# Residual parked in memory during the experts stage, its SBUF room used as a second buffer for one up matrix

## The chip, the cores and the metric

The kernel runs on one core of one Trainium2 chip. The metric is the device time of one execution in microseconds (us), as a median over runs. TensorE, VectorE, ScalarE and GpSimd are called PE, DVE, ACT and POOL in profile rows. SP is the engine whose queue issues nearly all transfers, and PS is the accumulator memory (PSUM).

## The reference, cut to what matters

The program is three blocks on one sequence of T = 512 tokens of width D = 1024, all in float32. The change lies in the last part of the first block, the mixture of experts:

```
x = x + gt1 * hybrid_mixer(...)                  # the residual
h = modulate(rmsnorm(x, g_norm2), sh2, sc2)
g = argmax(softmax(h @ w_rg + b_rg))             # one group of 4
e = top_k(softmax((h @ w_re + b_re)[g]), 2)      # two of its 8 experts
y[t] = sum_e w[t,e] * ((silu(h_t @ w_gate[e]) * (h_t @ w_up[e])) @ w_down[e])
x = x + gt2 * y                                  # the residual is needed again
x = rmsnorm(x, g_final)
```

There are 32 experts, each with a gate (1024 x 512), an up (1024 x 512) and a down matrix (512 x 1024), 2 MB each, so the stage reads 192 MB of weights, whatever the routing. Two more blocks follow (a gated delta rule with a feed-forward part, and an attention with one).

## The kernel before

**Pairs.** The experts stage works on two experts at a time. `PAIRS` is 16, and a hardware loop on each engine runs over "doubles", two pairs a turn (q = 0 and q = 1), eight turns for these inputs. For a pair PE does, in order: the gate product (`main_of`, line 874, 32 matmuls for two times 64 rows; `rest_of`, line 883, 32 for 32 more rows of the first expert), the up product (the same two lines), some transposes (lines 905, 864, 867 and 910, of the hidden rows and of the next pair's tokens), and the down product (line 919, 32 matmuls, and line 926, 32). Each ends with an increment of `m_pc`, six a pair: gate main, gate rest, up main, up rest, down main, down rest. `m_done(i, step)` is the value that `m_pc` has behind a step of pair i.

**Buffers.** A is one tensor of 59 rows of 512 floats per partition; an expert matrix takes eight rows. Gate matrices have two sets of buffers (lines 303 and 304): A[8:16] and A[16:24] for q = 0 and the two slots of `ring` for q = 1. Up matrices have one set, A[0:8] and A[32:40], and down matrices one set, A[24:32] and `h`. x is an SBUF tensor of 2 MB that holds the residual; during the stage nobody reads or writes it.

**Order of transfers.** SP issues all expert matrices from one queue. Ahead of the stage (lines 472 to 488): both gates of pair 0, the ups of pair 0, the first gate of pair 1 and the first down of pair 0; then the four writes of the token rows to `h2_tokens` (line 484, each behind its `ht_ev`); then a wait for the gathers of the token rows of pairs 0 and 1 (`xg`, line 486), the second down of pair 0 and the second gate of pair 1. In the loop (lines 508 to 522) each group of loads waits on `m_pc` until PE is through with the product that used the buffer: the gates of pair p+2 behind the gate product of pair p, the ups of p+1 behind the up product of p, the downs of p+1 behind the down product of p. PE waits for `wg`, `wu` and `wd` ahead of each product (lines 892, 899, 915).

**POOL** gathers token rows from `h2_tokens` for each pair by indirect DMA (line 2608) behind the `f_tok` semaphore, and writes finished rows to `y_assignments` (line 2646).

**Behind the stage** (lines 528 to 538) SP waits for the last hidden rows (`m_sg`) and gathers, loads `w_ab` and the first two weight units of the next block into `ring`, waits for the last writes of `y_assignments` (`sc0`, `sc1`), and loads these rows in four parts of 1 MB (line 538). DVE first takes the low parts of the first unit (line 2213), weighs and adds the rows part by part (lines 2224 and 2225), PE transposes them (line 933), and DVE adds them to the residual (line 2233): `x = PS * mod + x`.

Of the kernel before, what the change touches and what calls it, by code (L numbers as in the profile page):

```python
# [19 lines left out]
F32 = mybir.dt.float32  # L20
# [3 lines left out]
P = 128  # L24
D = 1024
T = 512
KD = D // P
NT = T // P
# [123 lines left out]
def build(nc, xt_in, wada, wall, wexp, w_if, w_router, w_ab, vecs, rows, b_if, cst_in, ints, att_bias, out_t):  # L152
    f_tok = nc.dram_tensor("h2_tokens", [T, D], F32, kind="Internal").ap()
    y_asg = nc.dram_tensor("y_assignments", [2 * T, D], F32, kind="Internal").ap()
    slots = nc.dram_tensor("slot_table", [SLOT_COLS * P, 2], I32, kind="Internal").ap()

    ctx = ExitStack()
    with ctx:
        def sb(name, shape, dt=F32):
# [4 lines left out]
        def S(name):  # L164
            if name not in sems:
                sems[name] = ctx.enter_context(nc.semaphore(name))
            return sems[name]
# [15 lines left out]
        h = sb("h", [P, KD, T])  # L183
        ring = sb("ring", [P, 2, 8, 512])
        A = sb("A", [P, 59, 512])
        x = sb("x", [P, KD, T])
# [113 lines left out]
        token_scale = A[:, 23, :]  # L300


        moe_up, moe_dn = [A[:, 0:8], A[:, 32:40]], [A[:, 24:32], h[:]]
        moe_gate = [[A[:, 8:16], A[:, 16:24]], [ring[:, 0], ring[:, 1]]]
        xg = [[A[:, 40:42, :], A[0:QUARTER, 42:44, :]], [A[:, 55:57, :], A[0:QUARTER, 57:59, :]]]
        x_main, x_rest = A[:, 44:46, :], A[:, 46, 0:KD * QUARTER]
# [13 lines left out]
        def m_done(i, step):  # L320

            return PRODUCTS * i + (step + 1)

        def rwait(eng, sem, value):

            eng.wait_ge(sem, value)
            eng.sem_inc(S("waits"), 1)
# [92 lines left out]
        def _(sp):  # L420
# [42 lines left out]
            def gate_of(q, j, e):  # L463
                sp.dma_start(moe_gate[q][j], e[:, 0].rearrange("a p k n -> p (a k) n")).then_inc(S(f"wg{q}{j}"), 16)

            def up_of(j, e):
                sp.dma_start(moe_up[j], e[:, 1].rearrange("a p k n -> p (a k) n")).then_inc(S(f"wu{j}"), 16)

            def down_of(j, e):
                sp.dma_start(moe_dn[j], e[:, 2].rearrange("a p k n -> p (a k) n")).then_inc(S(f"wd{j}"), 16)  # L470
# [1 line left out]
            sp.wait_ge(S("mm"), TILE_DONE[G_MOUT + 1][3])  # L472
            gate_of(0, 0, wexp[0:1])
            gate_of(0, 1, wexp[1:2])
            up_of(0, wexp[0:1])
            sp.wait_ge(S("merged"), KD)
            up_of(1, wexp[1:2])
            sp.wait_ge(S("mm"), UNIT_USED["w_out0"])
            gate_of(1, 0, wexp[2:3])
            sp.wait_ge(S("mm"), UNIT_USED["w_out1"])  # L480
            down_of(0, wexp[0:1])
            for t in range(NT):
                sp.wait_ge(S("ht_ev"), t + 1)
                sp.dma_start(f_tok[t * P:(t + 1) * P, :], A[:, 40 + 2 * t:42 + 2 * t, :].rearrange("p a b -> p (a b)")).then_inc(S("f_tok"), 16)
            for q in range(2):
                sp.wait_ge(S(f"xg{q}"), 32)
            down_of(1, wexp[1:2])
            gate_of(1, 1, wexp[3:4])

            n = doubles(sp)  # L490
            m = doubles_less_one(sp)
# [11 lines left out]

            def ups(es):
                for j in range(2):
                    up_of(j, es[j])

            with sp.Fori(1, n) as d:
                done = 2 * PRODUCTS * d
                before, first, second = experts(2 * d - 1), experts(2 * d), experts(2 * d + 1)  # L510
                rwait(sp, S("m_pc"), done + m_done(-2, 1))
                gates(0, first)
                rwait(sp, S("m_pc"), done + m_done(-2, 3))
                ups(before)
                rwait(sp, S("m_pc"), done + m_done(-2, 5))
                downs(before)
                rwait(sp, S("m_pc"), done + m_done(-1, 1))
                gates(1, second)
                rwait(sp, S("m_pc"), done + m_done(-1, 3))
                ups(first)  # L520
                rwait(sp, S("m_pc"), done + m_done(-1, 5))
                downs(first)
            last = experts(2 * m + 1)
            rwait(sp, S("m_pc"), 2 * PRODUCTS * m + m_done(0, 3))
            ups(last)
            rwait(sp, S("m_pc"), 2 * PRODUCTS * m + m_done(0, 5))
            downs(last)
            rwait(sp, S("m_sg"), 8 * n)
            for q in range(2):
                rwait(sp, S(f"xg{q}"), 32 * n + 32)  # L530
            sp.dma_start(wab[:], w_ab).then_inc(S("small2"), 16)
            for u in range(NU1, NU1 + 2):
                sp.dma_start(ring[:, u % 2], wall[u]).then_inc(S(f"unit{u % 2}"), 16)
# [44 lines left out]
        def _(pe):  # L578
# [75 lines left out]
            for k in range(KD):  # L654
                pe.wait_ge(S("h_lo"), k + 1)
                last = product(PS[0:64, 4, :], (wif_hi[:, k, :], wif_lo[:, k, :]), (x_r[:, k, :], h_r[:, k, :]), k == 0, k == KD - 1)
# [33 lines left out]
            for g in range(10):  # L690
# [3 lines left out]
                for j in range(4):  # L694
                    p = 4 * g + j
# [7 lines left out]
                    if j < 2 and g in (0, 2, 4, 8):  # L703
                        n = (0, 2, 4, 8).index(g)
# [165 lines left out]
            def main_of(bank, w):  # L870

                for k in range(KD):
                    for j in range(2):
                        last = mm(PS[HALF * j:HALF * (j + 1), bank, :], x_main[:, k // 4, (k % 4) * P + HALF * j:(k % 4) * P + HALF * (j + 1)],  # L874
                                  w[j][:, k, :], start=k == 0, stop=k == KD - 1)
                last.then_inc(S("m_pc"), 1)

            def rest_of(w):

                for k in range(KD):  # L880
                    for half in range(2):
                        g = HALF * (k % 2) + QUARTER * half
                        last = mm(PS[g:g + QUARTER, 5, 0:256], x_rest[:, k * QUARTER:(k + 1) * QUARTER], w[0][:, k, 256 * half:256 * (half + 1)],  # L883
                                  start=k < 2, stop=k >= KD - 2)
                last.then_inc(S("m_pc"), 1)

            rows_T(0, 32)
            n = doubles(pe)
            with pe.Fori(0, n) as d:
                for q in range(2):  # L890
                    for j in range(2):
                        pe.wait_ge(S(f"wg{q}{j}"), 16 * d + 16)
                    pe.wait_ge(S("m_x"), 4 * d + (2 * q + 1))
                    main_of(3, moe_gate[q])
                    pe.wait_ge(S("m_x"), 4 * d + (2 * q + 2))
                    pe.wait_ge(S("m_y1"), 2 * d + (q + 1))
                    rest_of(moe_gate[q])
                    for j in range(2):
                        pe.wait_ge(S(f"wu{j}"), 32 * d + 16 * (q + 1))
                    main_of(4, moe_up)  # L900
                    pe.wait_ge(S("m_h"), 8 * d + (4 * q + 1))
                    rest_of(moe_up)
                    pe.wait_ge(S("m_h"), 8 * d + (4 * q + 2))
                    for k in range(4):
                        last = nc.tensor.transpose(PS[:, 3, k * P:(k + 1) * P], hid_main[:, k * P:(k + 1) * P], ident)
                    last.then_inc(S("m_tr"), 1)
                    rows_T(1 - q, 32 * d + 32 * (q + 1))
                    rwait(pe, S("m_h"), 8 * d + (4 * q + 4))
                    for k in range(2):
                        last = nc.tensor.transpose(PS[:, 4, k * HALF:(k + 1) * HALF], hid_rest[:, k * P:(k + 1) * P], ident[0:HALF, 0:HALF])  # L910
                    last.then_inc(S("m_tr"), 1)
                    pe.wait_ge(S("m_ht"), 2 * d + (q + 1))
                    pe.wait_ge(S("m_y0"), 2 * d + (q + 1))
                    for j in range(2):
                        pe.wait_ge(S(f"wd{j}"), 32 * d + 16 * (q + 1))
                    for half in range(2):
                        for k in range(4):
                            for j in range(2):
                                last = mm(PS[HALF * j:HALF * (j + 1), 6 + half, :], hT_main[:, k * P + HALF * j:k * P + HALF * (j + 1)],  # L919
                                          moe_dn[j][:, 4 * half + k, :], start=k == 0, stop=k == 3)  # L920
                    last.then_inc(S("m_pc"), 1)
                    pe.wait_ge(S("m_hr"), 2 * d + (q + 1))
                    for k in range(4):
                        at = HALF * (k % 2) + QUARTER * (k // 2)
                        for t in range(4):
                            last = mm(PS[QUARTER * t:QUARTER * (t + 1), 5, 256:512], hT_rest[:, at:at + QUARTER],
                                      moe_dn[0][:, 4 * (t // 2) + k, 256 * (t % 2):256 * (t % 2 + 1)], start=k == 0, stop=k == 3)
                    last.then_inc(S("m_pc"), 1)
# [858 lines left out]
        def _(dve):  # L1787
# [240 lines left out]
            for m in range(2):  # L2028
                for j in range(4):
                    q = 8 + 4 * m + j  # L2030
# [162 lines left out]
            n = doubles(dve)  # L2193
# [32 lines left out]
            def a_lo(k):  # L2226

                dve.wait_ge(S("h_hi"), KD * (1 + MIX_SETS) + k + 1)
                stt(h_r[:, k, :], x[:, k, :], gm[:, 0, k:k + 1], h_hi_r[:, k, :].bitcast(F32), ALU.mult, ALU.subtract).then_inc(S("h_lo"), 1)

            for k in range(KD):
                dve.wait_ge(S("yT"), k + 1)
                stt(x[:, k, :], PS[:, k, :], mod[:, 40 + k:41 + k], x[:, k, :], ALU.mult, ALU.add).then_inc(S("xt"), 1)
                if k:
                    dve.wait_ge(S("xt"), KD + k)
                    a_lo(k - 1)
# [535 lines left out]
```

## Time and profile before

| | |
|---|---|
| median of 3 runs | 2365.41 us (2361.35 to 2365.88) |
| the profiled execution | 2357.39 us, of it the span 2355.5 us |
| PE busy | 2184.1 us (93%), mean granted clock 0.961 |
| DVE, ACT, POOL busy | 1212.3, 821.6, 107.0 us |
| moved by DMA | 384.62 MB, mean 163 GB/s |
| experts stage | roughly 470 to 966 us of the span |

In the rows below times are us from the start of the span; PEclk is the TensorE clock that was granted, as a share of 2.4 GHz, and the DMA share is the mean busy share of the core's 16 DMA engines.

### The profile page before, as it was taken

The page shows a single profiled execution, that of the slowest core. Times are in us where ns is not written, and L with a number is a line of the kernel's source. Part 1 is how long each engine was busy: PE and PEld are TensorE (multiplying, and loading weights), DVE is VectorE, ACT ScalarE, POOL GpSimd, SP SyncE. Part 2 cuts the span into 40 slices and gives each one's busy share as a digit, 9 for nine tenths or more (in the row PEclk, how much of TensorE's full clock was granted, in tenths as well). Part 3 has the DMA queues.
Part 4 walks back from the last instruction along what each step waited for, and adds up shares of the span by engine and source line. Part 5 has one row for each costly group of instructions (what it writes and reads, how often), then busy time and mean ns, then how long its engine had stood idle before and what let it go on. Part 6 is the DMA issues. An engine that isn't in the chain of part 4 may idle for free.

```text
span 2355.5 us, 30115 instructions
## 1 busy us (share of the span) xinstructions
PE 2184.1 (93%) x11752; PEld 1567.1 (67%) x11752; DVE 1212.3 (51%) x1813; ACT 821.6 (35%) x1494; POOL 107.0 (5%) x135
## 2 busy tenths in 40 slices
PE   7999998899998999799994989999999899999997
PEld 3788757633333343367783977888887677888885
DVE  4899576400000000457747446778525654877822
ACT  3222353233322333443552433223324454222421
POOL 0000000021111111000002000000000000000000
PEclk9999999899999999899996899999999899999999
DMA  9442104599999998511210112322223102222221
GB/s 393 169 179 77 71 33 164 201 387 428 426 426 424 418 418 354 206 72 72 72 37 1 37 58 86 107 77 102 108 107 112 68 1 96 84 107 107 76 104 72
DMA packets 34455, 384.62 MB, mean 163 GB/s; under 512 B 8112, under 2 KB 8384, under 8 KB 11456
## 3 DMA queue, kind: packets, MB, share of 16 engines
q1 hardware_dynamic: 27520, 374.96, 40.0%
q0 software_dynamic: 6848, 8.45, 1.0%
q8 instruction: 60, 0.98, 0.2%
q14 instruction: 27, 0.22, 0.0%
HBM read 382.59 MB, written 14.73 MB: 169 GB/s over the span
## 4 chain that ended last, share of the span: by engine, by line
PE 74%; DMA 13%; DVE 8%; ACT 4%; issue 2%; SPq 0%; DVEq 0%; ACTq 0%; POOL 0%; POOLq 0%
PE PS L646 19%; PE PS L647 18%; PE PS L648 18%; DMA A<-wexp 11%; PE PS L874 6%; PE PS L883 2%; DVE A L1903 1%; PE PS L919 1%; DMA x<-xt_in 1%; PE PS L1049 1%; PE PS L599 1%; PE PS L606 1%; PE PS L964 1%; PE PS L1242 1%; PE PS L626 0%
## 5 line engine op out<-in xcount | busy, mean ns | idle before, releaser
L647 PE MATMUL PS<-h_r,w_hi_r 128*128 128x512 f32 x1104 | 434.3, 393 | 0.0
L646 PE MATMUL PS<-h_hi_r,w_hi_r 128*128 128x512 f32 x1056 | 425.4, 403 | 8.9 <-DVE A L1903 3.4
L2213 DVE TENSOR_TENSOR ring_r<-ring,w_hi_r 128x1024 fp32r<-128x1024 f32 x196 | 238.7, 1223 | 345.1 <-ACT w_hi_r L1506 344.9
L648 PE MATMUL PS<-h_hi_r,ring_r 128*128 128x512 f32 x1056 | 414.9, 393 | 0.0
L1506 ACT ACTIVATE w_hi_r<-ring 128x1024 fp32r<-128x1024 f32 x196 | 206.2, 1058 | 567.9 <-PE PS L648 335.9
L646 PEld LDWEIGHTS PS<-h_hi_r,w_hi_r 128*128 128x128 f32 x1056 | 200.6, 190 | 63.5 <-issue 11.0
L647 PEld LDWEIGHTS PS<-h_r,w_hi_r 128*128 128x128 f32 x1104 | 210.3, 191 | 47.4 <-issue 4.8
L648 PEld LDWEIGHTS PS<-h_hi_r,ring_r 128*128 128x128 f32 x1056 | 200.8, 190 | 42.8
L874 PE MATMUL PS<-A 128*64 128x512 f32 x768 | 174.9, 609 | 25.9 <-DMA A<-wexp 23.9
L1903 DVE SCALAR_TENSOR_TENSOR A<-A,vec 128x511 f32<-128x511 f32 (+15 forms) x216 | 160.2, 742 | 6.7
L2198 DVE TENSOR_TENSOR A<-A,PS 64x256 f32<-64x256 f32 x16 | 6.6, 413 | 280.3 <-ACT A L1482 280.3
L874 PEld LDWEIGHTS PS<-A 128*64 128x64 f32 x768 | 59.6, 140 | 130.5 <-issue 128.4
L647 PE MATMUL PS<-hid_r,w_hi_r 128*128 128x512 f32 x352 | 136.9, 389 | 0.0
L646 PE MATMUL PS<-x_r,top_r 128*128 128x512 f32 x320 | 127.6, 399 | 5.6 <-DVE ring_r L1813 5.6
L647 PE MATMUL PS<-h_r,top_r 128*128 128x512 f32 (+1 forms) x328 | 128.9, 393 | 0.0
L648 PE MATMUL PS<-x_r,ring_r 128*128 128x512 f32 x320 | 125.8, 393 | 0.0
L919 PE MATMUL PS<-A 128*64 128x512 f32 x256 | 113.2, 595 | 0.3 <-DMA h<-wexp 0.3
L919 PE MATMUL PS<-h,A 128*64 128x512 f32 x256 | 113.3, 595 | 0.0
L1331 ACT ACTIVATE top_r<-ring 128x1024 fp32r<-128x1024 f32 x40 | 42.4, 1060 | 161.8 <-PE PS L648 161.8
L648 PE MATMUL PS<-h_r,ring_r 128*128 128x512 f32 x224 | 87.8, 392 | 0.0
L646 PE MATMUL PS<-top_r,w_hi_r 128*128 128x512 f32 x208 | 80.9, 389 | 0.0
L648 PE MATMUL PS<-top_r,ring_r 128*128 128x512 f32 x208 | 80.9, 389 | 0.0
(478 smaller groups left out, 3409.5 us busy)
## 6 DMA issues: line engine op xcount, KB each, us to landing
A<-wexp SPq DMA_DIRECT2D x64, 2048.0 KB, 15.8
ring<-wall SPq DMA_DIRECT2D x63, 2048.0 KB, 8.1
ring<-wexp SPq DMA_DIRECT2D x16, 2048.0 KB, 18.2
h<-wexp SPq DMA_DIRECT2D x16, 2048.0 KB
A<-wada SPq DMA_DIRECT2D x12, 2048.0 KB, 14.6
x<-xt_in SPq DMA_DIRECT2D x2, 2048.0 KB, 10.4
A<-y_assignments SPq DMA_DIRECT2D x4, 1024.0 KB, 7.8
h_tokens<-A SPq DMA_DIRECT2D x4, 512.0 KB, 3.0
```

The source lines that it names most:

```text
L599: mm(PS[:, bank, :], ones, sq[:, k % 2, :], start=k == 0, stop=k == KD - 1).then_inc(S("sq_used"), 1)
L606: last = mm(PS[g:g + QUARTER, NORM_BANK[n], :], ones[:, 0:QUARTER], A[:, k, :], start=k < 4, stop=k >= 4)
L646: mm(out, w[0], x_[0], start=first, stop=False)
L647: mm(out, w[0], x_[1], start=False, stop=False)
L648: return mm(out, w[1], x_[0], start=False, stop=last_)
L874: last = mm(PS[HALF * j:HALF * (j + 1), bank, :], x_main[:, k // 4, (k % 4) * P + HALF * j:(k % 4) * P + HALF * (j + 1)], w[j][:, k, :], s ...
L883: last = mm(PS[g:g + QUARTER, 5, 0:256], x_rest[:, k * QUARTER:(k + 1) * QUARTER], w[0][:, k, 256 * half:256 * (half + 1)], start=k < 2, s ...
L919: last = mm(PS[HALF * j:HALF * (j + 1), 6 + half, :], hT_main[:, k * P + HALF * j:k * P + HALF * (j + 1)], moe_dn[j][:, 4 * half + k, :], ...
L1331: a_(in_hi(p), ring[:, g % 2, :, j * P:(j + 1) * P], ACT.Copy).then_inc(S("w_hi"), 1)
L1506: a_(w_hi_r[:, :, j * P:(j + 1) * P], ring[:, slot, :, j * P:(j + 1) * P], ACT.Copy).then_inc(S("w_hi"), 1)
L1903: ins = stt(dst[:, s:T], src[:, 0:T - s], w(j), dst[:, s:T], ALU.mult, ALU.add)
L2213: tt(ring_r[:, slot, :, cols], ring[:, slot, :, cols], w_hi_r[:, :, cols].bitcast(F32), ALU.subtract).then_inc(S("w_lo"), 1)
```

## The change

The residual x is written to a DRAM tensor `x_kept` ahead of the token rows. Its room becomes the up buffer of the first expert for q = 1; the second expert's up matrix stays in A[32:40] for both q. Ahead of the loop SP now also loads the first up matrix of pair 1. In the loop the first up matrix of the following odd pair is issued right behind the ups of the even pair, so ahead of that even pair's downs; at the odd pair's turn only the second up matrix is loaded. Behind the stage x is read back, ahead of `w_ab`, and DVE waits for it before it adds.

```diff
+    x_kept = nc.dram_tensor("x_kept", [P, KD, T], F32, kind="Internal").ap()
...
-        moe_up, moe_dn = [A[:, 0:8], A[:, 32:40]], [A[:, 24:32], h[:]]
+        moe_up, moe_dn = [[A[:, 0:8], A[:, 32:40]], [x[:], A[:, 32:40]]], [A[:, 24:32], h[:]]
...
-            def up_of(j, e):
-                sp.dma_start(moe_up[j], e[:, 1].rearrange("a p k n -> p (a k) n")).then_inc(S(f"wu{j}"), 16)
+            def up_of(q, j, e):
+                sp.dma_start(moe_up[q][j], e[:, 1].rearrange("a p k n -> p (a k) n")).then_inc(S(f"wu{j}"), 16)
...
             down_of(0, wexp[0:1])
+            sp.wait_ge(S("xt"), KD)
+            sp.dma_start(x_kept, x[:]).then_inc(S("x_in"), 16)
             for t in range(NT):
                 sp.wait_ge(S("ht_ev"), t + 1)
...
             gate_of(1, 1, wexp[3:4])
+            sp.wait_ge(S("x_in"), 48)
+            sp.wait_ge(S("ht_mm"), NT)
+            up_of(1, 0, wexp[2:3])
...
             def ups(es):
                 for j in range(2):
-                    up_of(j, es[j])
+                    up_of(0, j, es[j])
...
                 rwait(sp, S("m_pc"), done + m_done(-2, 3))
-                ups(before)
+                up_of(1, 1, before[1])
...
                 rwait(sp, S("m_pc"), done + m_done(-1, 3))
                 ups(first)
+                up_of(1, 0, second[0])
                 rwait(sp, S("m_pc"), done + m_done(-1, 5))
                 downs(first)
...
             rwait(sp, S("m_pc"), 2 * PRODUCTS * m + m_done(0, 3))
-            ups(last)
+            up_of(1, 1, last[1])
...
+            sp.dma_start(x[:], x_kept).then_inc(S("x_in"), 16)
             sp.dma_start(wab[:], w_ab).then_inc(S("small2"), 16)
...
-                    main_of(4, moe_up)
+                    main_of(4, moe_up[q])
                     pe.wait_ge(S("m_h"), 8 * d + (4 * q + 1))
-                    rest_of(moe_up)
+                    rest_of(moe_up[q])
...
+            dve.wait_ge(S("x_in"), 64)
             for k in range(KD):
                 dve.wait_ge(S("yT"), k + 1)
                 stt(x[:, k, :], PS[:, k, :], mod[:, 40 + k:41 + k], x[:, k, :], ALU.mult, ALU.add).then_inc(S("xt"), 1)
```

## Rows read from the trace of the kernel before

**Rows 1.** The page: the span in 40 slices, and the chain that ended last.

```profile
PE   7999998899998999799994989999999899999997
DMA  9442104599999998511210112322223102222221
GB/s 393 169 179 77 71 33 164 201 387 428 426 426 424 418 418 354 206 72 72 72 37 1 37 58 86 107 77 102 108 107 112 68 1 96 84 107 107 76 104 72
PE 74%; DMA 13%; DVE 8%; ACT 4%; issue 2%; SPq 0%; DVEq 0%; ACTq 0%; POOL 0%; POOLq 0%
```

**Rows 2.** Waits of PE, 484 to 960 us: waited for, us in total, times, longest.

```profile
PE PS L874 <- DMA A<-wexp: 23.9, 12, 3.2
PE PS L919 <- DMA h<-wexp: 0.3, 1, 0.3
```

**Rows 3.** Timeline of PE: start, us, what [idle before <-releaser].

```profile
570.95 7.09 PE L874 MATMUL PS<-A 128*64 128x512 f32 x32 [0.87 <-DMA A<-wexp]
...
726.32 7.09 PE L874 MATMUL PS<-A 128*64 128x512 f32 x32 [2.84 <-DMA A<-wexp]
...
822.45 8.78 PE L874 MATMUL PS<-A 128*64 128x512 f32 x32 [3.06 <-DMA A<-wexp]
...
853.83 7.09 PE L874 MATMUL PS<-A 128*64 128x512 f32 x32 [0.63 <-DMA A<-wexp]
...
865.40 0.61 PE L919 MATMUL PS<-A 128*64 128x512 f32 x1 [0.29 <-DMA h<-wexp]
...
917.30 7.09 PE L874 MATMUL PS<-A 128*64 128x512 f32 x32 [2.27 <-DMA A<-wexp]
...
928.51 0.64 PE L919 MATMUL PS<-A 128*64 128x512 f32 x1
```

**Rows 4.** Timeline of SP's queue: issues of transfers.

```profile
895.20 0.85 SPq L467 DMA_DIRECT2D A<-wexp  x2
906.41 0.33 SPq L470 DMA_DIRECT2D A<-wexp  x1
906.92 0.33 SPq L470 DMA_DIRECT2D h<-wexp  x1
926.52 0.86 SPq L467 DMA_DIRECT2D A<-wexp  x2
...
956.39 0.90 SPq L533 DMA_DIRECT2D ring<-wall  x2
971.25 0.80 SPq L538 DMA_DIRECT2D A<-y_assignments  x2
```

**Rows 5.** Windows: us, busy of PE, PEld, DVE, ACT, POOL, PEclk, DMA share, GB/s.

```profile
482.00:484.00 2.00, 2.00 (x30) 0.76 (x22) 0.38 (x1) 0.38 (x1) 0.00 (x0) 1.00 0.67 275
484.00:486.00 2.00, 2.00 (x12) 0.70 (x10) 0.04 (x1) 0.42 (x1) 0.89 (x2) 1.00 0.72 123
486.00:488.00 2.00, 2.00 (x12) 0.72 (x10) 0.00 (x0) 0.00 (x0) 0.24 (x1) 1.00 0.57 238
...
492.00:568.00 76.00, 76.00 (x550) 30.36 (x546) 5.57 (x13) 28.49 (x75) 15.13 (x21) 1.00 1.01 426
568.00:918.00 350.00, 325.81 (x2392) 134.41 (x2392) 24.86 (x56) 110.95 (x289) 47.90 (x68) 0.99 1.01 423
918.00:922.00 4.00, 4.00 (x20) 1.55 (x18) 0.00 (x0) 0.00 (x0) 0.00 (x0) 1.00 0.41 164
922.00:926.00 4.00, 4.00 (x44) 1.63 (x40) 0.69 (x1) 0.00 (x0) 0.00 (x0) 1.00 0.11 45
926.00:927.00 1.00, 1.00 (x15) 0.82 (x8) 0.27 (x1) 0.51 (x2) 0.00 (x0) 1.00 0.00 0
...
968.00:970.00 2.00, 0.00 (x0) 0.00 (x0) 0.00 (x0) 1.97 (x3) 0.90 (x1) 1.00 0.49 162
```

**Rows 6.** Issue and landing of the second gate of pair 1, issued at 471.40 us.

```profile
ring<-wexp SPq DMA_DIRECT2D x1, 2048.0 KB, 13.4
```

**Rows 7.** Landing of the token-row write issued last, at 454.57 us; POOL's first gather behind it.

```profile
h_tokens<-A SPq DMA_DIRECT2D x1, 512.0 KB, 3.2
463.95 1.24 POOL L2608 DMA_INDIRECT A<-h_tokens,idx  x1 [122.31 <-DVE idx L2156]
```

**Rows 8.** Timeline of DVE behind the stage, the first part of the rows.

```profile
976.08 0.75 DVE L2224 TENSOR_SCALAR A<-A,wtok 128x1024 f32<-128x1024 f32 x1 [0.42 <-DMA A<-y_assignments]
```

More of the change, by code:

```diff
@@ L474, in _ @@
             gate_of(0, 1, wexp[1:2])
-            up_of(0, wexp[0:1])
+            up_of(0, 0, wexp[0:1])
             sp.wait_ge(S("merged"), KD)
-            up_of(1, wexp[1:2])
+            up_of(0, 1, wexp[1:2])
             sp.wait_ge(S("mm"), UNIT_USED["w_out0"])
```

## The prediction

> **What bounds the kernel now.** I read the page first. Over the whole span PE is busy and carries 74% of the chain, but the slices around the experts are different: the DMA engines stand at 9 tenths and 387 to 428 GB/s for eight slices [rows 1]. So one stage of a PE kernel is bound by transfers. The windows confirm it: from 568 to 918 us the share is 1.01 at 423 GB/s [rows 5]. In PE's waits, every idle stretch from 484 to 960 us is a wait for an expert matrix: 12 waits for an up matrix, 23.9 us, and one of 0.3 us for a down matrix [rows 2]. From 492 to 568 us PE is busy throughout, although the share is already 1.01 [rows 5]: there PE is the slower one and lives on what was loaded ahead. The first wait stands at 570.95, the last at 917.30 us [rows 3], and from the last up product on PE runs through to the stage's end. Between those two starts lie eleven pairs, 66 matrices, in 346.35 us: **5.25 us a matrix**, token rows and results included. So the stage's end is set by when the up matrices of pair 14 land and by the PE work behind them.
>
> The queue is worked off in order. The ups of pair 14 were issued at 895.20 and let PE start at 917.30; the downs, issued at 906.41 and 906.92 [rows 4], were still moving at 922 to 926 us, with a share of 0.11, which is under two of 16 engines, and at 926 to 927 nothing moved [rows 5]. Two readings follow: a matrix counts as landed when the slowest engine is through, some 7 us behind the others, and downs land about 8.8 us behind ups at the tail. The Trainium skill (DMA: Bandwidth & Descriptors, Queues, rings and completion order) says that each engine consumes a queue's descriptors in ring order and that the semaphore needs all of them; the tail agrees.
>
> A down matrix has almost no slack. Pair 12's ups let PE start at 853.83, and its down product started at 865.40 after a wait of 0.29 us [rows 3]: PE needs the downs 11.2 to 11.5 us after it starts the ups (928.51 - 917.30 = 11.21 in pair 14), and two matrices behind the ups take 2 x 5.25 = 10.5.
>
> **The change, part by part.**
>
> *The write of x* (2 MB, SBUF to memory) stands in the queue ahead of the token-row writes. Its wait on `xt` is over at about 445 us, when x is final, and the first token write is issued at 451, so SP itself loses nothing. On the engines it costs 4.9 us (2.1 MB at 423 to 428 GB/s). The last token write landed at 454.57 + 3.2 = 457.8; with the write in front, at 462.7. POOL's gather started at 463.95, released by DVE's indices about 1 us earlier [rows 7]. Cost 0, hidden by the routing arithmetic; the cover is 0.3 us, so the bound above is what is left if writes run slower: 0 to +2, and a rival beyond it. The Trainium skill (DMA: Bandwidth & Descriptors, Anatomy of one DMA) warns that the receipt of a write to HBM dominates a transfer's fixed time; it speaks against a write in front of others here, but the 3.2 us of a 512 KB write in rows 7 holds that already.
>
> *The first up matrix of pair 1, loaded ahead.* It follows the second gate of pair 1, which landed at 471.40 + 13.4 = 484.8 [rows 6]. The next loads, the gates of pair 2, began to move after 485; the windows from 482 to 488 show shares of 0.67, 0.72 and 0.57 at 275, 123 and 238 GB/s [rows 5]. The idle room that the early load can use is between 1.4 us (slowest engine, my estimate from the landing less its receipt) and 2.9 us (bytes missing from 482 to 488 against 423 GB/s). I take 1.4, since landings go by the slowest engine. Everything behind it shifts by 5.25 - 1.4 = +3.9 us (2.3 to 4.9).
>
> *What this does in the saturated loop.* Counting matrices ahead of each product from 484 us on: ahead of any pair's **ups** the queue now carries one matrix less than before, so they land 5.25 - 3.9 = 1.4 us earlier. Ahead of an even pair's **downs** it carries as many as before (one went ahead of the stage, but the next odd pair's first up matrix was put in front of them), so these land 3.9 us later. Ahead of an odd pair's downs one less: 1.4 earlier. The early lead therefore buys nothing where it counts: the even downs, with 0 to 2.6 us of slack (landed by about 925.9, used at 928.51), become the wait that decides. Each even pair then waits about 3 x 5.25 - 11.3 = 4.5 us for its downs, and the waits on ups go nearly to nothing. The engines stay fed: each group of loads is still issued several us before the queue runs dry, so the period per pair stays 31.5 us.
>
> *The last even pair, 14.* Its downs landed at 925.9 and now land at 925.9 + 3.9 = 929.8, PE starts them at 930.0: **+1.5 us**. From the other side: ups at 915.8 and three matrices behind them, at the tail's 4.4 us 929.0, at 5.25 us 931.6, so +0.5 to +3.1. All behind is PE work that no longer waits (pair 15's second up and downs have 10 us to spare), so it shifts by the same.
>
> *The clock.* A wait of 2.84 us or less left the next 32 matmuls at 7.09 us, one of 3.06 made them 8.78: the clock had fallen from 2.4 to 1.2 GHz, 1.69 us [rows 3]. In pairs 4 to 12 the longer waits will do this with no cost, DMA being the bound. In pair 14 the wait is 930.0 - (915.9 + 11.2) = 2.9 us, on the edge. I charge half, **+0.85** (0 to +1.7).
>
> *Reading x back.* 2 MB go ahead of `w_ab` and two ring units, issued at 956.0 to 957.3 [rows 4]. These were through at about 969.3 (share 0.49 in 968 to 970) [rows 5] and will be at 974.2. The parts of the rows are issued at 971.25, began to move at about 972.4, and DVE took the first at 976.08, after a wait for it of 0.42 [rows 8]; now they begin at 974.4. **+2.0 us**, between 0 (if the engines take them in between) and the whole 4.9. ACT splits the first unit at 969.5, which then has just landed: 0. DVE's new wait on `x_in` is met by then: 0.
>
> *PE, DVE and ACT work* is unchanged; three more issues on SP of 0.33 to 0.43 us stand in stretches in which SP waits: 0.
>
> Sum: 0 + 1.5 + 0.85 + 2.0 = **+4.4 us**. Against the profiled execution, 2357.39, that is 2361.8; this execution lies 8.0 us under the median of the runs, 2365.41, so in terms of the median **2369.8 us**.
>
> **The rivals.**
>
> A, the forecast: even downs decide, the reading back costs part of itself. +1 to +8 us.
>
> B, **not slower**: the lead reaches the end. It decides if the downs of pair 14 had more room than the last moving engine shows, that is, if they land under 928.5 in spite of the matrix in front. Then only the 1.4 us earlier ups count, or up to a whole matrix, 5.25, if the engines' idle room at 484 was as long as that; with the reading back hidden: -5.25 to 0, 2360.2 at best, 2363 if half. For it: the mean of the engines was through at 919, seven us before the last. Against it: the 0.29 us wait of pair 12, and the order of issue. The Trainium skill (DMA: Bandwidth & Descriptors, Rules for kernel authors) says to issue a transfer early and wait for it late. By that rule alone the early load is a gain.
>
> C, the write of x holds up the token rows. It decides once the write takes over 5.2 us. At half the rate of the loads it takes 9.8, and gathers, first pair and loop all begin 4.6 us later: 2374. For it: the 0.3 us of cover. Against it: the token writes ran at nearly the loads' rate.
>
> D, the end costs more: the last writes of `y_assignments` now share the engines with the ring loads, so the parts are issued late and the whole 4.9 us shows, with the clock's 1.7 in full: +1.5 + 1.7 + 4.9 = +8.1, 2373.5.
>
> That the change doesn't do what it says is part of A: the second buffer serves only one up matrix of every second pair.
>
> **How the numbers follow.** About 0.2% (4.7 us) is what a measurement of this kernel can tell. Chances: A 0.55, of it 0.30 within 0.2% and 0.25 slower, for 4.4 us lies on that edge and most bounds lie above; B 0.20, of it 0.12 faster and 0.08 the same; C 0.10 and D 0.15, both slower. In all: faster 0.12, same 0.38, slower 0.50. The range goes from 2363 (half of B) to 2377 (C with D's end); A's own is 2366.4 to 2373.4.
>
> **What would show it.** In the changed trace: waits of PE on line 919 of 3 to 5 us in seven even pairs, few on line 874; the first of them in pair 2 (about 552 us) and the last in pair 14 at 930; a mean of 31.5 us a pair as before; the first gather of POOL still at 464; DVE's first use of the parts 2 us later against the end of the stage. Wrong would be: no waits on line 919 (B), a gather at 466 or later (C), parts 5 us later (D), or a period other than 31.5 us.

## The result, and the profile after

The changed kernel takes 2370.87 us (median of 10 runs, 2369.93 to 2371.41), the kernel before 2361.78 us in its 10 runs beside them (the three that stood ahead of the prediction are among them). The ratio is 1.0039, 95% interval 1.0030 to 1.0048: slower by 9.1 us. Those three had a median 3.6 us above that of the ten, so the forecast of 2369.8 lay close to the measured time partly by this offset; as a difference it was +4.4 against +9.1. One execution of e5 below took 10877.63 us; it is taken for a disturbed run and left out of the ratio.

The profiled executions differ by 14.0 us (spans 2355.5 and 2369.5), since that of before, at 2357.39 us, lies under all ten of its timed runs and that of the changed kernel, at 2371.41, is the slowest of its ten. I read them for where the time went, and take sizes from the timed runs.

The page of the changed kernel: the DMA share, rates and the chain, to be held against [rows 1].

```profile
DMA  9442104599999998611210012222222102222221
GB/s 392 167 178 81 70 28 179 224 396 426 414 420 410 412 416 345 259 50 57 81 63 1 33 40 107 87 90 106 107 107 107 71 1 81 97 106 106 72 107 71
PE 78%; DMA 9%; DVE 8%; ACT 4%; issue 1%; SPq 0%; DVEq 0%; ACTq 0%; POOL 0%; POOLq 0%
```

The stage still looks bound by transfers, but from the eleventh slice on it moves 410 to 420 GB/s where it moved 418 to 426. The waits of PE from 484 to 980 us (waited for: us, times, longest) have changed their line, as forecast:

```profile
PE PS L928 <- DMA h<-wexp: 22.0, 7, 3.7
PE PS L883 <- DMA A<-wexp: 0.5, 1, 0.5
```

Line 928 is the down product now, line 883 the main product of gate and up. Twelve waits for ups have become seven for downs, one in each even pair from 2 to 14 [rows 2]. They are 1.5 to 3.7 us long, where 3 to 5 were forecast. The timeline of PE shows the first, those of pairs 4 and 8, and the last (start, us, what, idle before it):

```profile
556.13 0.61 PE L928 MATMUL PS<-A 128*64 128x512 f32 x1 [1.49 <-DMA h<-wexp]
...
617.52 1.08 PE L928 MATMUL PS<-A 128*64 128x512 f32 x1 [3.36 <-DMA h<-wexp]
...
744.18 1.09 PE L928 MATMUL PS<-A 128*64 128x512 f32 x1 [3.64 <-DMA h<-wexp]
...
921.16 7.09 PE L883 MATMUL PS<-A 128*64 128x512 f32 x32 [0.45 <-DMA A<-wexp]
935.96 0.61 PE L928 MATMUL PS<-A 128*64 128x512 f32 x1 [3.52 <-DMA h<-wexp]
```

Pair 14's down product starts at 935.96, 7.45 us later than at 928.51 [rows 3]. Of these, 4.66 are there in pair 4 already, whose down product began in the kernel before at

```profile
612.86 0.64 PE L919 MATMUL PS<-A 128*64 128x512 f32 x1
```

The other 2.8 come in the ten pairs from 4 to 14, which take 31.84 us each in place of 31.57. So the period did change, which the forecast had named as a sign of being wrong. The windows of the changed kernel from 504 on (columns as in [rows 5]) show why transfers fell behind:

```profile
502.00:504.00 2.00, 2.00 (x16) 0.57 (x16) 0.00 (x0) 0.07 (x1) 0.00 (x0) 1.00 1.02 426
504.00:508.00 4.00, 4.00 (x44) 1.57 (x35) 0.00 (x0) 2.45 (x5) 1.05 (x1) 1.00 0.56 123
508.00:510.00 2.00, 2.00 (x12) 0.72 (x10) 0.00 (x0) 0.00 (x0) 1.11 (x2) 1.00 0.88 360
```

and the same hole in a later odd pair:

```profile
754.00:758.00 4.00, 4.00 (x41) 1.56 (x34) 0.00 (x0) 2.38 (x5) 1.04 (x1) 1.00 0.64 201
758.00:760.00 2.00, 2.00 (x12) 0.72 (x10) 0.00 (x0) 0.00 (x0) 1.10 (x2) 1.00 1.00 410
```

In the kernel before, the window that answers to the first hole reads

```profile
504.00:508.00 4.00, 4.00 (x22) 1.35 (x20) 0.00 (x0) 0.94 (x3) 1.80 (x4) 1.00 0.98 399
```

The queue runs dry. At 505.85 SP issues the downs of pair 1 into buffers that PE has only then released, and the loads ahead of them are nearly through by 504. The hole is worth (399 - 123) x 4 = 1.1 MB, 2.6 us.

Part of this hole belongs to this execution and not to the change. The first gate product of pair 0, first in the kernel before and then in the changed one, took

```profile
472.81 8.47 PE L874 MATMUL PS<-A 128*64 128x512 f32 x32 [2.00 <-ACT A L1466]
```

```profile
473.76 9.85 PE L883 MATMUL PS<-A 128*64 128x512 f32 x32 [2.00 <-ACT A L1475]
```

since the granted clock stayed at 1.2 GHz for longer (0.50 in its first 4 us, where it was 0.65). So the down buffers came free later, and pair 1's downs were issued 54.4 us behind the first write of token rows, in the kernel before 52.2. The profiles of e3, e4 and e5 below have the same loop, a first product of 8.5 to 8.6 us, and these downs at 52.6 to 52.9. From 48 to 62 us behind that write they moved 369 to 372 GB/s, the changed kernel 323 and the kernel before 425. By these numbers 1.4 MB are missing in these 14 us, of which the load ahead costs about 0.8, 1.8 us, and the slow first product the rest. That product was slow (9.6 to 10.1 us) in five of the six profiles with the write of x in front of the token rows, and in one of the seven others. Whether the write has a part in it is open.

In the odd pairs behind, a hole comes again (share 0.64 from 754 to 758), now because the even downs are late: their product ends late, their buffers come free late, and the odd pair's downs are issued late, here at 755.80.

Over the saturated middle this adds up. First the kernel before, then the changed one:

```profile
600.00:880.00 280.00, 261.69 (x1891) 108.09 (x1892) 20.01 (x45) 89.04 (x233) 37.83 (x52) 0.99 1.00 422
```

```profile
600.00:880.00 280.00, 263.00 (x1866) 104.21 (x1864) 20.01 (x45) 87.12 (x229) 35.75 (x50) 0.95 0.99 416
```

6 GB/s over 280 us are 1.7 MB, about 4 us of transfers; and the granted clock fell from 0.99 to 0.95, since most down products run at the 1.2 GHz level for a while behind their waits. In pair 14 that is on the path:

```profile
937.00:939.00 2.00, 2.00 (x8) 0.83 (x6) 0.00 (x0) 0.00 (x0) 0.00 (x0) 0.50 0.18 74
```

The issues of SP show that this down product released its buffers at 946.89, 9.15 us later than at 937.74, so 1.7 us were added to the 7.45.

```profile
946.89 0.33 SPq L472 DMA_DIRECT2D A<-wexp  x1
...
965.16 0.33 SPq L539 DMA_DIRECT2D x<-x_kept  x1
...
966.00 1.84 SPq L542 DMA_DIRECT2D ring<-wall  x2
985.23 0.80 SPq L547 DMA_DIRECT2D A<-y_assignments  x2
```

Then the end. From the first load of the end to the issue of the row parts it was 971.25 - 956.01 = 15.24 us and is 985.23 - 965.16 = 20.07: +4.8. The chain of waits names the reason, the last write of rows. Before, then after (start, us):

```profile
969.06 1.96 DMA y_assignments<-A,sidx
```

```profile
978.19 6.80 DMA y_assignments<-A,sidx
```

The write starts 13.0 us behind the first load of the end both times. It used to find the engines nearly done with the ring units, and now stands among their packets. The windows behind its start, before and after:

```profile
970.00:972.00 2.00, 0.00 (x0) 0.00 (x0) 1.44 (x2) 2.00 (x3) 0.00 (x0) 0.64 0.02 4
```

```profile
978.00:980.00 2.00, 0.00 (x0) 0.00 (x0) 0.00 (x1) 1.69 (x3) 0.90 (x1) 0.50 0.95 360
```

SP waits for it and issues the parts 4.8 us later. At the front, POOL's first gather starts 0.9 us later:

```profile
464.83 1.28 POOL L2618 DMA_INDIRECT A<-h_tokens,idx  x1 [122.99 <-DVE idx L2165]
```

In the profiles: 9.15 + 4.8 = 14.0 us, the difference of the spans.

### The profile page after: what moved, and what is told of

Same layout as the page of the kernel before. It is cut to its first block, busy times and chain, and to the rows that moved or that the text cites. A ratio compares the mean times of both kernels' runs of the same rounds, so it can differ in the third digit from the quotient of the medians.

```text
span 2369.5 us, 30117 instructions
## 1 busy us (share of the span) xinstructions
PE 2194.7 (93%) x11752; PEld 1566.6 (66%) x11752; DVE 1212.0 (51%) x1813; ACT 821.6 (35%) x1494; POOL 107.1 (5%) x135
## 4 chain that ended last, share of the span: by engine, by line
PE 78%; DMA 9%; DVE 8%; ACT 4%; issue 1%; SPq 0%; DVEq 0%; ACTq 0%; POOL 0%; POOLq 0%
PE PS L655 18%; PE PS L657 18%; PE PS L656 18%; DMA h<-wexp 7%; PE PS L883 5%; PE PS L928 5%; PE PS L892 1%; PE PS L935 1%; DVE A L1912 1%; DMA x<-xt_in 1%; PE PS L1058 1%; PE PS L608 1%; PE PS L615 1%; PE PS L973 1%; PE PS L1251 1%
## 5 line engine op out<-in xcount | busy, mean ns | idle before, releaser
L883 PE MATMUL PS<-A 128*64 128x512 f32 x640 | 172.8, 605 | 2.5 <-ACT A L1475 2.0
L928 PE MATMUL PS<-A 128*64 128x512 f32 x256 | 125.5, 648 | 22.0 <-DMA h<-wexp 22.0
L928 PE MATMUL PS<-h,A 128*64 128x512 f32 x256 | 125.6, 648 | 0.0
L883 PEld LDWEIGHTS PS<-A 128*64 128x64 f32 x640 | 53.3, 139 | 74.5 <-issue 69.4
L928 PEld LDWEIGHTS PS<-A 128*64 128x64 f32 x256 | 36.7, 149 | 94.6 <-issue 94.0
```

## The experiments

All times are ratios to runs of the kernel before on the same chip, turned into us at 2360. For each profile I also took two stretches from SP's issues: **stage**, from the first write of token rows to the first load behind the loop, and **end**, from there to the issue of the row parts. These two are of single executions, whose totals scatter by several us: the changed kernel's stage is 2.8 us longer than in e4, e5 and e8, which have the same loop.

| kernel | ratio (95%) | us against before | stage | end |
|---|---|---|---|---|
| before | 1 | 0 | 504.7 | 15.2 |
| changed | 1.0039 (1.0030 to 1.0048) | +9.2 | 513.8 | 20.1 |
| e1 downs first | 1.0017 (1.0008 to 1.0026) | +4.0 | 505.8 | 19.6 |
| e2 park only | 1.0022 (1.0014 to 1.0031) | +5.2 | 507.7 | 19.5 |
| e3 no park | 1.0018 (1.0010 to 1.0027) | +4.2 | 510.2 | 15.2 |
| e4 tokens first | 1.0041 (1.0029 to 1.0053) | +9.7 | 511.0 | 19.9 |
| e5 second unit last | 1.0020 (1.0011 to 1.0029) | +4.7 | 511.0 | 15.2 |
| e6 three edits | 0.9991 (0.9983 to 1.0000) | -2.1 | 503.5 | 15.2 |
| e7 before, second unit last | 1.0002 (0.9993 to 1.0011) | +0.5 | 505.7 | 15.2 |
| e8 x last | 1.0026 (1.0014 to 1.0037) | +6.1 | 511.0 | 15.2 |
| e9 one buffer | 0.9995 (0.9986 to 1.0005) | -1.2 | 507.9 | 15.2 |
| e10 ahead of the ups | 1.0059 (1.0045 to 1.0073) | +13.9 | 512.0 | 19.4 |
| e11 three edits again | 0.9998 (0.9989 to 1.0006) | -0.5 | 505.0 | 15.2 |

### The order in the queue

e1 undoes one thing:

```diff
                 ups(first)
-                up_of(1, 0, second[0])
                 rwait(sp, S("m_pc"), done + m_done(-1, 5))
                 downs(first)
+                up_of(1, 0, second[0])
```

> The changed kernel, but in the loop the first up matrix of the odd pair is issued behind the even pair's downs, no longer ahead of them. Theory Q (the order in the queue makes the even downs late; their lateness also lowers PE's clock and empties the queue, since the next downs are issued late): waits on the down product at line 928 go from 7 (22.0 us) to at most 1, waits on the up product at line 883 come back (10 or more), the DMA share no longer falls to 0.5 to 0.7 in each odd pair, the matmuls of pair 14's down product take 7.0 us again in place of 8.8. The down product of pair 14 then starts 4 to 6 us earlier, and the time is 5 to 8 us below the changed kernel's 2370.9: 2363 to 2366. Rival R (the loop loses through its buffers or through x as a target, whatever the order): the time stays at 2369 or more, and the waits merely change their line.

Measured: +4.0 us over before in place of +9.2. That is 5.2 us gained where 5 to 8 were expected, and the median of its runs is 2363.97. The waits of PE in e1:

```profile
PE PS L883 <- DMA A<-wexp: 21.9, 11, 3.0
PE PS L928 <- DMA h<-wexp: 0.8, 3, 0.3
```

The middle of the stage is fed again:

```profile
600.00:880.00 280.00, 262.55 (x1918) 108.86 (x1914) 19.99 (x45) 89.64 (x234) 37.49 (x52) 0.99 1.00 423
```

So the order alone makes the late downs, the dry queue in the odd pairs and the low clock. Three waits for downs are left where at most one was expected, none over 0.3 us. The hole at the start of the loop is not cured (0.41 at 160 GB/s from 507 to 509 us): it comes from the load ahead itself, and in this execution also from a first product of 9.98 us. e10 goes the other way, one place further ahead:

```diff
-                ups(first)
                 up_of(1, 0, second[0])
+                ups(first)
```

(the x buffer's load has a semaphore of its own there, since two loads in flight on one semaphore could be taken for each other).

> The changed kernel with the odd pair's first up matrix moved one place further ahead, in front of the even pair's ups (on a semaphore of its own). Theory Q (the even downs are late because one matrix more stands ahead of them): they are exactly as late, since the same matrices stand ahead; the even ups are now 5 us later too, so PE's waits split between lines 883 and 928 with about the same sum (20 to 26 us), and the time stays within 2 us of the changed kernel, 8 to 10 us above the kernel before. Each wait is shorter, so fewer down products run at the low clock. Rival (what costs is the single long wait ahead of the down product and the low clock behind it): 3 us or more under the changed kernel.

Measured +13.9 us (10.6 to 17.2), no gain anywhere, so the rival falls. But 8 to 10 were expected, and the waits were neither split nor shorter: with the ups late too, PE waits for them alone, up to 4.5 us, and the downs are back inside their 11 us.

```profile
PE PS L883 <- DMA A<-wexp: 24.4, 7, 4.5
```

That it is some us slower than the changed kernel I did not follow up; its profiled execution, at 2369.85, doesn't show it.

### What parking costs

e3 leaves out the write of x and the reading back, and with them the residual in the last addition. e2 keeps both and gives up the second buffer, and with it the load ahead and the new order.

```diff
# e3
-            sp.wait_ge(S("xt"), KD)
-            sp.dma_start(x_kept, x[:]).then_inc(S("x_in"), 16)
...
-            sp.dma_start(x[:], x_kept).then_inc(S("x_in"), 16)
# e2
-        moe_up = [[A[:, 0:8], A[:, 32:40]], [x[:], A[:, 32:40]]]
+        moe_up = [[A[:, 0:8], A[:, 32:40]], [A[:, 0:8], A[:, 32:40]]]
```

> The changed kernel without the write of x and without the reading back (so the residual is lost and the last addition of the stage uses weights in its place). Theory: the loop alone is left. First gather at 464.0, seven waits of 3 to 4 us on the down product, the end of the stage as long as in the kernel before; time 5 to 6 us under the changed kernel: 2365 to 2366, so still 3 to 4 us above the kernel before. Rival (the whole loss is in the two ends): time of the kernel before, within 1 us.

> The changed kernel with the write of x and the reading back kept, but with the one set of up buffers and the order of loads of the kernel before. Theory P (what parking costs by itself is its two ends): first gather 0.9 us later than in the kernel before, the loop as before (12 waits for ups, none over 0.5 us for downs), the parts of the rows 4.8 us later against the end of the stage; in all 5 to 6 us above the kernel before, 2367 to 2368. Rival (the two ends are hidden, as half of my sum had it): 2 us or less above.

Measured: e3 +4.2 us where 3 to 4 were expected, e2 +5.2 where 5 to 6 were. The two add up to 9.4, the changed kernel's 9.2: within the scatter of the timed runs loop and parking add up, and are nearly equal. The end of e3, issued as in the kernel before, 978.94 - 964.09 + 0.39 = 15.24 us:

```profile
963.70 0.34 SPq L536 DMA_DIRECT2D wab<-w_ab  x1
964.09 0.90 SPq L538 DMA_DIRECT2D ring<-wall  x2
978.94 2.10 SPq L543 DMA_DIRECT2D A<-y_assignments  x4
```

The front is not where the expectation put it: e3's first gather starts 20.2 us behind the issue of the last load ahead of the token rows, without any write in front. e4 asks the same directly:

> The changed kernel with the write of x issued behind the four writes of token rows. Theory: the token rows land at 458 as in the kernel before, the first gather starts at 464.0 in place of 464.8 and the whole rest follows, 0.9 us less: 2370.0. Rival (the gather started late because of the routing work on PE and DVE and its clock, not of the write): no change, 2370.9. With the write behind, its packets share the engines with the gathers, which could cost up to 1 us back.

Measured +9.7 (6.8 to 12.5) against +9.2: no gain to be seen. From that last load (line 470, later 472) to the gather it is 19.66, 20.15, 20.17, 19.65, 20.09, 20.17 and 19.74 us in before, e3, e4, e6, e7, e9 and e11, with nothing in front, and 20.41, 20.84, 20.17, 20.15, 20.21 and 20.43 in the changed kernel, e1, e2, e5, e8 and e10, with the write in front. That is 0.4 us on average, and less than the scatter of a timed run. Only in e10 does the profile name the token write as what released POOL:

```profile
465.52 1.35 POOL L2618 DMA_INDIRECT A<-h_tokens,idx  x1 [123.17 <-DMA h_tokens<-A]
```

So the forecast's 0 to +2 with a cover of 0.3 us holds for the gather.

The end has the cost. e5 moves the second ring unit behind the parts, e8 moves x there, and e7 makes e5's edit in the kernel before:

```diff
-            for u in range(NU1, NU1 + 2):
+            for u in range(NU1, NU1 + 1):
                 sp.dma_start(ring[:, u % 2], wall[u]).then_inc(S(f"unit{u % 2}"), 16)
...
                 sp.dma_start(A[:, 4 * t:4 * t + 4, :], y_asg...[t]).then_inc(S(f"to_A{t}"), 16)
+            sp.dma_start(ring[:, 1], wall[NU1 + 1]).then_inc(S("unit1"), 16)
```

> The changed kernel with the load of the second ring unit behind the stage issued after the four parts of the rows, not ahead of them (x, w_ab, first unit, parts, second unit). Theory E (the reading back costs its end because it makes the row of transfers ahead of the last writes of y_assignments and of the parts 4.9 us longer): from the issue of x to the issue of the parts 15 to 16 us in place of 20.1, and 4 to 5 us less in all, 4.5 to 5.5 us above the kernel before. Rival (the last writes land late for another reason, or DVE or PE waits for the second unit instead): less than 2 us gained, 7 or more above the kernel before.

> The changed kernel with the reading back of x issued behind the four parts of the rows. The parts are then issued 15.2 us after the first load of the end, as in the kernel before, and x lands 5 us after the last part, so DVE's last addition waits 2 to 3 us for it: 1.5 to 3 us less than the changed kernel, 6 to 8 above the kernel before.

> The kernel before with one edit, the second ring unit loaded behind the parts of the rows. In the kernel before the last write of rows lands 2 us after its issue and the parts are issued right behind it, so the second unit is nearly hidden there: 0 to 1 us gained. If the last writes were held up by it already, 2 us or more gained.

Measured +4.7 us for e5, +6.1 for e8 and +0.5 for e7. The first two are within what was written; e7 was expected to gain 0 to 1 us, and its interval, -1.7 to +2.6, allows that but doesn't show it. In e8 DVE waits for x, as it must:

```profile
997.00 1.41 DVE L2243 SCALAR_TENSOR_TENSOR x<-PS,mod,x 128x512 f32<-128x512 f32 x2 [2.80 <-DMA x<-x_kept]
```

e7 says that in the kernel before the second unit was hidden, to within that interval, and e5 that 4.5 us are charged as soon as one more 2 MB load stands in front of it.

### What the second buffer is worth

> Three edits of the changed kernel together: downs ahead of the next odd pair's first up matrix, token rows ahead of the write of x, second ring unit behind the parts. If the costs are the ones found (queue order, long end) and the second up buffer is worth nothing in itself, it comes to the kernel before, within 1.5 us. If the buffer has a worth that was hidden under the costs, it is 2 us or more under the kernel before.

e6 came out at 0.9991 (0.9983 to 1.0000), on the edge between the two. So it was run again, beside the same kernel with one set of up buffers:

> The kernel of the three edits, but with the one set of up buffers and the order of loads of the kernel before: x is still written behind the token rows and read back, the second ring unit still comes last. Against the three edits this gives what the second up buffer is worth by itself. Theory W0 (nothing: the load ahead only makes the engines idle later, between pair 1's second up and its downs, whose buffers PE still holds): within 1 us of the three edits and of the kernel before. Theory W2 (the buffer keeps the engines fed at the start of the loop): 1.5 to 3 us above the three edits.

> The kernel of the three edits once more, for the comparison with one set of buffers on the same chip, and to see whether it is below the kernel before: 0 to 2 us below.

e11 gives 0.9998 (0.9989 to 1.0006) and e9 0.9995 (0.9986 to 1.0005). With both edits of the ends and the queue in order, a kernel with the second buffer and one without take the same time, and both take that of the kernel before. The twelve runs of each scatter so much that a difference of about 2 us either way would not be told, so a worth of 1.5 us stays possible and is not shown; one of more than 3 us is not compatible with them. No version was shown to beat the kernel before. e6's windows show where the lead goes:

```profile
504.00:506.00 2.00, 2.00 (x20) 0.72 (x14) 0.00 (x0) 1.21 (x4) 1.05 (x1) 1.00 0.88 230
506.00:508.00 2.00, 2.00 (x14) 0.59 (x10) 0.00 (x0) 0.29 (x1) 0.80 (x1) 1.00 0.62 229
```

The load ahead fills the engines from 482 to 488 us (419, 410 and 438 GB/s, in the kernel before 275, 123 and 238), and at 504 to 508 they stand partly idle instead, because the next loads, the downs of pair 1, need buffers that PE gives back at 504.86 and no earlier. In e2 and e9, without the load ahead, the window from 504 to 508 moves 426 and 420 GB/s. The exchange isn't complete: from 30 to 62 us behind the first write of token rows e6 moves 397 GB/s and the kernel before 385, so some 0.4 MB, 0.9 us of lead, are left, less than the timed runs can tell.

## Why the prediction was right and wrong

**The bound and the place** were read rightly: a stage bound by transfers, one matrix more ahead of each even pair's downs, waits moving from the ups to the downs, first in pair 2 (at 556 us, forecast at 552), last in pair 14, seven in all, and no gain to be seen from the load ahead. e1, at +4.0, is no slower than parking alone (e2, +5.2), so this one order is the loop's whole loss, as far as the timed runs tell.

**The write of x**, 0 (0 to +2): right; at most a few tenths.

**Pair 14's downs**, +1.5 (+0.5 to +3.1): mis-sized, 7.45 us in the profiles, and the loop's part is 4 to 5 us in the timed runs (e3 +4.2; the changed kernel less e1, 5.2). The step that failed is the sentence "The engines stay fed", and with it "the period per pair stays 31.5 us": the odd pair's downs are issued at 755.80, when the share has already fallen, and the period from pair 4 to 14 is 31.84 us. The queue was reckoned for the slowest engine at 5.25 us a matrix and never for the others, which by [rows 5] are some 7 us ahead at the tail. Two holes follow, of which neither was in the sum: one from 504 on, of which 1.8 us come from the load ahead, and in each odd pair a shorter one, together about 4 us from 600 to 880. How these make up the 7.45 isn't shown. (The bytes missing from 482 to 488 us come to 3.0 us of transfers and not to 2.9, which changes no term of the sum.)

**The clock**, +0.85: mis-sized, 1.7 us. From the start of pair 14's down product to the release of its buffers it is 9.23 us in the kernel before, and 10.68 to 10.93 in all five profiles with a wait there (changed, e3, e4, e5, e8), though the waits are 1.67 to 3.52 us. The edge at 3 us was read from waits ahead of up products and carried over to a wait ahead of a down product, where it doesn't hold, see below.

**Reading back**, +2.0 (0 to 4.9): mis-sized, 4.8 us. The sum let the parts wait for the engines, and not for the last write of rows, which the wait on `sc0` and `sc1` makes them do. That was rival D's mechanism. Its price of 4.9 was the right one.

**The rivals.** B falls: lead doesn't reach the end even with the costs removed (e9 beside e11). C falls (e4). D is half of the result, at a size of 4.5 to 4.8 us. Had D's end been in the sum, it would have been +7.2. The total came within 1.1 us of 2369.8 by luck: three terms were too small, and the median that they were added to was 3.6 us too high.

Still open is why e10 is slower than the changed kernel, and how the loop's loss divides between lateness and holes; the lateness and the odd pairs' holes both go away with e1's edit.

## What to carry to other kernels

In a stage bound by transfers like this one, ask of a buffer more whether the loads behind it can be issued earlier too; here they could not, and most of the idle time of the engines just moved to the next load that waited for its room. A load put ahead in a saturated queue delays the loads behind it, so look for the one with the least slack, and then for what its late use will release late. And where a queue of large loads precedes a small write that somebody waits for, one load more in front can show nearly in full (4.5 of 4.9 us here): put the loads that are needed last behind the wait.

## What the runs showed of the hardware

A small scattered write had no priority among large loads. The last write of rows took 1.96 us from its start on engines that were nearly idle and 6.80 us among the packets of one more load.

The granted clock doesn't fall at a fixed length of wait. After a wait of 2.25 us it had fallen in e9 and the 32 matmuls took 8.78 us:

```profile
921.58 8.78 PE L882 MATMUL PS<-A 128*64 128x512 f32 x32 [2.25 <-DMA A<-wexp]
```

while in e1 the same wait ahead of the same product left it at 2.4 GHz:

```profile
920.78 7.09 PE L883 MATMUL PS<-A 128*64 128x512 f32 x32 [2.25 <-DMA A<-wexp]
```

By the counts over all profiles, what PE did before the wait mattered as much as its length. Ahead of an up product stand the gate products; none of the 44 waits of up to 1.99 us there was followed by a slower product, 16 of the 36 from 2.2 to 3.0 us were, and 9 of the 10 longer ones; after one of 3.60 us, in e10, the product still ran at 2.4 GHz. Ahead of a down product stand short transposes; there 33 of the 35 waits of 1.49 to 5.01 us were followed by a slower product. The shortest of these is in e4, where the product starts at 2.4 GHz, falls, and releases its buffers 10.92 us after its start in place of 9.23:

```profile
935.89 0.61 PE L928 MATMUL PS<-A 128*64 128x512 f32 x1 [1.67 <-DMA h<-wexp]
...
937.00 1.06 PE L928 MATMUL PS<-A 128*64 128x512 f32 x1
```

So this kernel paid the clock wherever it moved its waits from the ups to the downs. Differences like that of 1.4 us in the first gate product may be a part of why its executions scatter by several us; no run shows how large a part.
